# Gate units interleaved with projection units, and late Gelu tiles put in one activation, in the recurrent layer of a two-block transformer kernel

## The reference, cut to what matters

```python
z = hn @ w_in                      # 1024 -> 2 * 1408
gate, xr = split(z, 2)
xr = causal_depthwise_conv(xr, conv_w, conv_b)     # 4 taps along the tokens
r = sigmoid(blockdiag(xr, gate_a_w) + gate_a_b)    # 16 blocks of 88
i = sigmoid(blockdiag(xr, gate_x_w) + gate_x_b)
log_a = -8 * r * softplus(-lam)
a = exp(log_a)
u = sqrt(-expm1(2 * log_a)) * (i * xr)
h = scan(h[t] = a[t] * h[t-1] + u[t])
y = (h * gelu(gate)) @ w_out
```

## Time and profile before

| what | value |
|---|---|
| median of the runs | 1759.29 us (1758.56 to 1760.14) |
| span of the profiled execution | 1760.3 us |
| TensorE busy (matmul) | 1679.2 us, 95% |
| VectorE busy | 1309.1 us, 74% |
| ScalarE busy | 821.5 us, 47% |
| GpSimd busy | 244.3 us, 14% |

### The profile page before, as it was taken

The page is one execution under the profiler, slowest core; times in us unless marked ns, Lnnn a source line. Parts: engine busy times, 40 slices in busy tenths (PEclk is TensorE's granted clock), DMA queues, the critical chain, the costliest instruction groups (busy, mean ns, idle before and its releaser), DMA issues.

```text
span 1760.3 us, 28611 instructions
## 1 busy us (share of the span) xinstructions
PE 1679.2 (95%) x11790; PEld 1508.8 (86%) x11790; DVE 1309.1 (74%) x1809; ACT 821.5 (47%) x1185; POOL 244.3 (14%) x199
## 2 busy tenths in 40 slices
PE   6999998999999999899999999969999999899999
PEld 3797776788778877887999999969999999799999
DVE  4678768888888878857477777887988868757453
ACT  3334652443224323546454556485635444456362
POOL 0323001011001112440310112013000220030000
PEclk9899999999999999999999999989999999999999
DMA  7633004233465558320246657634998966037552
GB/s 301 263 120 120 1 18 154 93 144 114 163 238 215 200 180 314 119 93 1 97 160 237 231 190 261 213 115 161 358 360 322 347 216 230 34 117 278 189 183 72
DMA packets 46576, 317.84 MB, mean 181 GB/s; under 512 B 5232, under 2 KB 6256, under 8 KB 12272
## 3 DMA queue, kind: packets, MB, share of 16 engines
q1 hardware_dynamic: 45936, 312.68, 49.2%
q0 software_dynamic: 512, 3.35, 0.5%
HBM read 314.96 MB, written 1.05 MB: 180 GB/s over the span
## 4 chain that ended last, share of the span: by engine, by line
PE 80%; DVE 12%; ACT 3%; issue 3%; POOL 2%; DMA 1%; DVEq 0%; ACTq 0%
PE PM L1615 22%; PE PM L1616 21%; PE PM L1617 21%; PE PO L1930 3%; DVE acc L1051 3%; PE PM L1890 2%; DVE wlo L1017 2%; PE PX L1914 2%; PE PX L1799 1%; PE PX L1588 1%; PE PX L1856 1%; DVE Hlo L1513 1%; PE PM L1699 1%; PE PM L1701 1%; DVE X L1198 1%
## 5 line engine op out<-in xcount | busy, mean ns | idle before, releaser
L1615 PE MATMUL PM<-Hhi,whi 128*128 128x256 f32 (+1 forms) x1686 | 526.8, 312 | 7.2 <-DVE Hlo L1439 1.9
L1616 PE MATMUL PM<-Hlo,whi 128*128 128x256 f32 (+1 forms) x1686 | 522.9, 310 | 0.0
L1617 PE MATMUL PM<-Hhi,wlo 128*128 128x256 f32 (+1 forms) x1686 | 522.8, 310 | 0.0
L1017 DVE TENSOR_TENSOR wlo<-raw,whi 128x2048 fp32r<-128x2048 f32 (+2 forms) x199 | 437.5, 2198 | 90.5 <-ACT whi L717 90.1
L717 ACT ACTIVATE whi<-raw 128x2048 fp32r<-128x2048 f32 (+3 forms) x204 | 365.4, 1791 | 133.8 <-PE PM L1617 95.2
L1615 PEld LDWEIGHTS PM<-Hhi,whi 128*128 128x128 f32 x1686 | 323.0, 192 | 32.9 <-issue 10.5
L1617 PEld LDWEIGHTS PM<-Hhi,wlo 128*128 128x128 f32 x1686 | 323.1, 192 | 16.6
L1616 PEld LDWEIGHTS PM<-Hlo,whi 128*128 128x128 f32 x1686 | 323.1, 192 | 15.8
L1615 PE MATMUL PM<-Ghi,whi 128*128 128x256 f32 (+1 forms) x864 | 265.2, 307 | 1.7 <-DVE X L1198 1.6
L1051 DVE SCALAR_TENSOR_TENSOR acc<-raw,silc,acc 128x512 f32<-128x512 f32 x356 | 265.2, 805 | 1.5 <-DVE X L1198 0.6
L1617 PE MATMUL PM<-Ghi,wlo 128*128 128x256 f32 (+1 forms) x864 | 263.2, 305 | 0.0
(11 more groups left out here) (220 smaller groups left out, 2304.5 us busy)
## 6 DMA issues: line engine op xcount, KB each, us to landing
raw<-in_ada SPq DMA_DIRECT2D x104, 1024.0 KB, 5.0
raw<-in_wm SPq DMA_DIRECT2D x93, 1024.0 KB, 5.1
raw<-in_wl SPq DMA_DIRECT2D x68, 1024.0 KB, 5.0
raw<-in_wl SPq DMA_DIRECT2D x32, 704.0 KB, 4.2
raw<-in_wm SPq DMA_DIRECT2D x5, 768.0 KB, 5.5
raw<-in_wm SPq DMA_DIRECT2D x4, 704.0 KB, 4.0
X<-in_x SPq DMA_DIRECT2D x1, 2048.0 KB, 11.8
bias<-in_bias POOLq DMA_DIRECT2D x1, 2048.0 KB, 11.0
```

The costliest lines, as they stand in the source:

```text
L1017: dve.tensor_tensor(wslot(wlo, i, usize(u)), slot_raw(n, usize(u)), wslot(whi, i, usize(u)).bitcast(F32), ALU.subtract)\
L1615: pe.matmul(out, st_hi, mv_hi, start=first, stop=False)
L1616: pe.matmul(out, st_hi, mv_lo, start=False, stop=False)
L1617: return pe.matmul(out, st_lo, mv_hi, start=False, stop=last)
```

## The change

The units of the recurrent layer get another order (`LORDER`): a gate unit follows as soon as the tiles that it needs have been projected. `lsplit` is gone; each XR tile is split at the step after its `lin` unit. It goes into columns 2048 to 4095 of Hhi and Hlo, a ring of eight tiles, in which tiles 8 to 10 wait for the gate unit that last used tiles 0 to 2. The Gelu of gate tiles 4 to 10 is not applied when they are taken out of PSUM; they are copied, and one Gelu over 1792 columns follows at `lin` 10. In each `lin` evacuation the conv tap now comes ahead of the gate tile. Two ada tiles move from `lin` 7 and 9 to `lin` 6 and 8, so that both stay with `lin` units. In unit numbers: 100 to 103 `lin` 0 to 3, 104 `lgate` 0, 105 and 106 `lin` 4 and 5, 107 `lgate` 1, 108 and 109 `lin` 6 and 7, 110 `lgate` 2, 111 to 113 `lin` 8 to 10, 114 to 116 `lgate` 3 to 5.

```diff
+LORDER = [("lin", 0), ("lin", 1), ("lin", 2), ("lin", 3), ("lgate", 0), ("lin", 4), ("lin", 5), ("lgate", 1), ("lin", 6), ("lin", 7),
+          ("lgate", 2), ("lin", 8), ("lin", 9), ("lin", 10), ("lgate", 3), ("lgate", 4), ("lgate", 5)]
+LGELU = 4
...
-                if key == ("lgate", 0):
-                    prog.append(("lsplit",))
...
-    for i in [*range(2, 6), *range(12, 24, 2), *range(24, 49), *range(74, 82, 2), 92, 94, 96, *range(101, 110, 2), *range(124, 153),
+    for i in [*range(2, 6), *range(12, 24, 2), *range(24, 49), *range(74, 82, 2), 92, 94, 96, 101, 103, 105, 108, 111, *range(124, 153),
...
+        def xtile(j):
+            return KD * 256 + (j % KD) * 256
+        def xtile_user(j):
+            n = max(g for g, js in enumerate(GATE_UNITS) if any(j in GATES[i] for i in js))
+            return first_of("lgate", "M0") if n == 0 else next(u["i"] for u in UNITS if u["kind"] == "lgate" and u["idx"] == n)
...
             def split_x(j):
                 act.wait_ge(*at("lxd", j))
-                act.activation(Hhi[:, j * 256:j * 256 + 256], XR[:, j * 256:j * 256 + 256], ACT.Copy).then_inc(*tick("hhi", ("x", j)))
+                if j >= KD:
+                    act.wait_ge(*at("unit", xtile_user(j - KD)))
+                o = xtile(j)
+                act.activation(Hhi[:, o:o + 256], XR[:, j * 256:j * 256 + 256], ACT.Copy).then_inc(*tick("hhi", ("x", j)))
...
                 elif kind == "lin":
                     j = u["idx"]
                     act.wait_ge(*at("unit", i))
-                    if j == NL - 1:
-                        for c in range(3):
-                            split_x(c)
-                    act.activation(GT[:, j * 256:j * 256 + 256], pm(i, 0, 256), ACT.Gelu_apprx_tanh).then_inc(*tick("pm_act", i))
                     act.activation(XR[:, j * 256:j * 256 + 256], pm(i, 512, 256), ACT.Identity, scale=fcol("lcw", 3 * NL + j),
                                    bias=fcol("lcb", j)).then_inc(*tick("lx", j))
+                    act.activation(GT[:, j * 256:j * 256 + 256], pm(i, 0, 256), ACT.Gelu_apprx_tanh if j < LGELU else ACT.Copy)\
+                        .then_inc(*tick("pm_act", i))
+                    if j == NL - 1:
+                        act.wait_ge(*at("pm_act", i))
+                        q = slice(LGELU * 256, NL * 256)
+                        act.activation(GT[:, q], GT[:, q], ACT.Gelu_apprx_tanh).then_inc(*tick("lg", 0))
...
                         split_hi(i + 2)
                     if up_before:
                         ffn_stage3(UNITS[i - 1])
+                    if i and UNITS[i - 1]["kind"] == "lin":
+                        split_x(UNITS[i - 1]["idx"])
                     evac(u)
```

More of the change, by code:

```diff
@@ L114, in make_units @@
                 add("down", st, h * KD + n, HALF, 128, T)
[L115 to L118, removed]
+    for kind, n in LORDER:
+        if kind == "lin":
+            add("lin", "M0", n, KD, 256, 256)
+        else:
+            add("lgate", "M0", n, 2 * sum(len(GATES[j]) for j in GATE_UNITS[n]), 128, 256)
     for n, ks in enumerate(LPARTS):
@@ L964, in _ @@
                     attn(step[1])
-                elif step[0] == "lsplit":
-                    for j in range(3, NL):
-                        split_x(j)
                 elif step[0] == "lscan":
@@ L1272, in split_x @@
                 dve.wait_ge(*at("hhi", ("x", j)))
-                dve.tensor_tensor(Hlo[:, j * 256:j * 256 + 256], XR[:, j * 256:j * 256 + 256], Hhi[:, j * 256:j * 256 + 256].bitcast(F32),
+                o = xtile(j)
+                dve.tensor_tensor(Hlo[:, o:o + 256], XR[:, j * 256:j * 256 + 256], Hhi[:, o:o + 256].bitcast(F32),
                                   ALU.subtract).then_inc(*tick("hlo", ("x", j)))
@@ L1760, in unit @@
                                 ins = three(pm(i, c * 512 + g * 256, 256), wslot(whi, i, 128, at_ * 128), wslot(wlo, i, 128, at_ * 128),
-                                            mh[:, ci * 256:ci * 256 + 256], ml[:, ci * 256:ci * 256 + 256], m == 0, m == len(GATES[j]) - 1)
+                                            mh[:, xtile(ci):xtile(ci) + 256], ml[:, xtile(ci):xtile(ci) + 256], m == 0, m == len(GATES[j]) - 1)
                                 at_ += 1
@@ L2079, in _lay_out @@
             pos += 1
-    seq = _units_of(f["lru_w_in_2"][0], KD, [np.concatenate([ar(j * P, j * P + P), LW + ar(j * P, j * P + P)]) for j in range(NL)])
+    lin = _units_of(f["lru_w_in_2"][0], KD, [np.concatenate([ar(j * P, j * P + P), LW + ar(j * P, j * P + P)]) for j in range(NL)])
     dense = []
@@ L2086, in _lay_out @@
         dense.append(m)
-    for js in GATE_UNITS:
-        seq.append(np.concatenate([dense[g][m * P:(m + 1) * P, j * P:(j + 1) * P] for j in js for g in range(2) for m in GATES[j]], axis=1))
+    lgate = [np.concatenate([dense[g][m * P:(m + 1) * P, j * P:(j + 1) * P] for j in js for g in range(2) for m in GATES[j]], axis=1)
+             for js in GATE_UNITS]
+    seq = [lin[n] if kind == "lin" else lgate[n] for kind, n in LORDER]
     wl = f["lru_w_out_2"][0]
```

## The result

The change made the kernel slower: 1764.68 us median (1763.11 to 1766.20, 7 runs) against 1759.29 (1756.10 to 1761.19, 7 runs), a ratio of 1.0028 with a 95% interval of 1.0018 to 1.0037. That is 4.9 us by the ratio, 5.4 by the medians: 0.3% of the kernel's time, small but clear of the noise. An execution's own time is 1.8 us over its span here (1763.49 and 1761.7 in the profiled one); the front matter took the span of before for its time, which does not touch the difference.

The account below looks back on a forecast made before the run. TensorE, busy 95% of the span, was taken as the bound. Waits and a clock fall end `lin` 10 at 1157.9; 15.6 of tail makes gate unit 4's Exp 4.6 us later: 1759.3 + 4.6, said as 1764.0, range 1758.5 to 1767.5.

Parts of the forecast that it names:

- The sum: Whole kernel: gate unit 4's Exp at 1173.5 against 1168.9, so the end 4.6 us later, said as 1764.0.
- The loop: Gate units 0 to 2: VectorE's order closes a loop from Exp to Exp of 17.1 to 17.2 us, against TensorE's 15.84.
- TensorE's waits: TensorE waits 2.4 us in gate unit 1, 1.0 in gate unit 2 and 2.1 at the ada sum before `lin` 10.
- The clock: `lin` 10: after the 2.1 us wait and 16 small matmuls TensorE's granted clock falls, adding 1.5 us.
- The tail: ScalarE's work from the end of `lin` 10 to gate unit 4's Exp, late Gelu and table loads included: 15.6 us.
- Hidden gates: Projection units take up the gate units' VectorE and ScalarE work, TensorE never waits: 2.9 us earlier, 1756.4; chance 0.19.
- A switch that empties ScalarE: Tail: each of two added table switches drains ScalarE, costing 2 x 1.28 us more, to 1766.6; chance 0.03.
- The clock stays up: `lin` 10: same waits but no half rate, 1.5 us less, 1762.4; chance 0.18.
- More falls of the clock: Half rate also after gate unit 1's wait, 1.1 us longer, and more in the tail: 1765.6 to 1767.5; chance 0.08.
- The large hole of 12.6 us: TensorE's wait for the first scan, before the filler matmuls; claimed hardly shortened, still 12 to 14 us.

Follow-up runs that it names:

- Run 1: Changed kernel with three ada tiles moved to gate units 0 to 2, multiplied before VectorE waits for the Exp; 1756.63 us, 0.9987 of the kernel before.
- run 2: Changed kernel with VectorE's gate work of gate units 0 to 2 put one unit later; 1769.91 us, 1.0065 of the kernel before.
- run 9: Changed kernel with 4 filler matmuls on TensorE ahead of the ada sum before `lin` 10; 1764.20 us, 1.0029 of the kernel before.
- run 3: Changed kernel with the late Gelu moved from `lin` 10 to behind the four square roots; 1763.19 us, 1.0020 of the kernel before.
- run 7: Changed kernel with a one-column Gelu at gate unit 4 on ScalarE, adding two table switches; 1766.64 us, 1.0041 of the kernel before.
- runs 6: Changed kernel with 15 filler matmuls on TensorE ahead of the ada sum before `lin` 10; 1767.27 us, 1.0047 of the kernel before.
- The best of them: Changed kernel with the late Gelu behind the square roots and ada tiles at gate units 1 and 2 and `lin` 10; 1755.21 us, 0.9984 of the kernel before.

## Why the prediction was right, point by point

- **The sum.** 4.6 us forecast for the way to the first scan, 4.70 measured; 1764.0 forecast, 1764.68 measured. That the stretch agrees to 0.1 is in part luck: it was taken in an execution in which the clock did not also fall in gate unit 1.
- **The loop.** Exp to Exp 17.2 and 16.9 forecast, 17.3 and 17.0 measured. (The prediction's own terms add up to 17.26, a little over the 17.1 to 17.2 that it states.) Run 1 took the loop away without taking work away and the loss went with it; run 2 made the loop longer and the loss larger. VectorE's idle time before the gate work was 1.8 to 1.9, forecast 1.7.
- **TensorE's waits.** 2.4, 1.0 and 2.1 forecast, 1.89, 0.77 and 2.02 measured. `lin` 10 was taken up 61.5 us after `lin` 3, as forecast (1157.9 + 0.26 - 1096.63), though the waits were 0.8 smaller in sum. The loop sets the moments and not the waits: with the 2.44 us added by which this execution was ahead, the Exps of gate units 1 and 2 ended at 1122.9 and 1139.9 and the ada sum began at 1149.5, where 1123.0, 1139.9 and 1149.5 were forecast.
- **The clock.** 1.5 us for `lin` 10, shown by run 9. It came there in every traced execution with that wait and no fillers. At the wait in gate unit 1, to which the prediction's sum gave nothing, it came in three of five and cost 0.7 to 0.9.
- **The tail.** From `lin` 10's first instruction to the end of gate unit 4's Exp 15.3 forecast (15.6 less the crossing), 15.5 measured; the late Gelu 1.70 as interpolated; three loads where three were expected. But "the tail" wasn't additive: run 3 shows that only 1.5 of its 4.3 us for the late Gelu and its two loads were on the path, Exp's load in full and the rest for 0.2, since TensorE's gate unit 3 stands right behind. My text listed them as full terms of the sum, and without this run a reader would expect 4.3 from removing them.
- **The rivals.** Hidden gates: the place that the prediction named decided against it, since tile 4 came 1.89 us late for gate unit 1's ninth block. A switch that empties ScalarE: excluded by run 7. The clock stays up: not in `lin` 10. More falls of the clock: happens in some executions.

The large hole of 12.6 us, the reason for such a change, was never on offer: it lies behind three gate units, which have no projection unit between them in any of these orders. The best of them took 1.2 from it.

## What to carry to other kernels

When units of different kinds are interleaved, don't compare sums of work with the period; write down, for each in-order engine, the loop that runs through the other engine's last instruction and back, and see whether it is longer. An idle wait in such a loop is best filled with work that nobody waits for soon (here a modulation tile; TensorE needs it only for a later sum), put ahead of the wait; moving the waiting work behind other work may only lengthen the loop. And a cost in a tail is worth only as much as the next engine's work behind it allows.

## What I had not expected of the hardware

A switch of ScalarE's table took 1.28 to 1.29 us in each of the places looked at, with the next activation right behind it. A wait of 1.9 us on TensorE at the same place was followed by half clock (0.50 for 3.2 us) in three executions (runs 6, 7 and 9) and by none in two (the changed kernel and run 3). And before the part that was changed, executions of the same instructions came to `lin` 3 between 1092.9 and 1096.6 us, so a difference of one or two microseconds of span says little; the stretch between two fixed events says it.
